# Paired channel tiles, convolution sums in PSUM, MLP weight sums on VectorE and a new GpSimd order in a one-layer hybrid decoder step

## The reference, cut to what matters

```python
def layer(x, s_pool, s_conv, p0, norm1_g, w_in, pool_w, pool_scale, conv_w, w_out, norm2_g, w1, w2):
    hn = rmsnorm(x, norm1_g)
    proj = jnp.einsum('btd,de->bte', hn, w_in)          # 1024 -> [u | B | C | h], 4 x 512
    ya, new_pool = pool_mixer(u, s_pool, p0, pool_w, pool_scale)   # causal means over 2, 4, 8, 16
    yb, new_conv = conv_mixer(bg, cg, hc, s_conv, conv_w)          # B * conv3(C * h)
    mix = jnp.concatenate([ya, yb], axis=-1)
    x = x + jnp.einsum('bte,ed->btd', mix, w_out)
    hn = rmsnorm(x, norm2_g)
    a = jax.nn.relu(jnp.einsum('btd,df->btf', hn, w1))  # 1024 -> 4096
    x = x + jnp.einsum('btf,fd->btd', a * a, w2)        # 4096 -> 1024
    return x, new_pool, new_conv
```

## Time and profile before

| | us |
|---|---|
| median of 3 runs | 713.3 |
| the three runs | 709.56, 713.3, 722.66 |
| the profiled execution | 708.97 |
| its span, slowest core | 707.4 (699.6 to 707.4 over the 8 cores) |
| PE busy | 630.9 (89%), 5430 matmuls |
| DVE busy | 523.2 (74%) |
| ACT busy | 303.9 (43%) |
| POOL busy | 204.6 (29%) |

### The profile page before, as it was taken

The page is one execution under the profiler, slowest core; times in us unless marked ns, Lnnn a source line. Parts: engine busy times, 40 slices in busy tenths (PEclk is TensorE's granted clock), DMA queues, the critical chain, the costliest instruction groups (busy, mean ns, idle before and its releaser), DMA issues.

```text
span 707.4 us, 13629 instructions; the slowest of 8 cores (699.6 to 707.4 us)
## 1 busy us (share of the span) xinstructions
PE 630.9 (89%) x5430; PEld 522.0 (74%) x5430; DVE 523.2 (74%) x1289; ACT 303.9 (43%) x816; POOL 204.6 (29%) x204
## 2 busy tenths in 40 slices
PE   4898896798899588899999996598999999999995
PEld 1486684587678477688888885377878888888895
DVE  2359889589989679737647549957895985976987
ACT  3443352254433345127146054103625735736734
POOL 7078497167638111100000006727220000000001
PEclk9999999899999799999999998799999999999998
DMA  8996295625249977961360466459930450420614
GB/s 211 165 197 143 31 227 143 225 70 184 40 144 192 166 106 215 323 215 35 138 213 5 179 200 110 103 155 184 228 134 2 138 216 2 160 87 1 215 33 123
DMA packets 33983, 100.05 MB, mean 141 GB/s; under 512 B 6720, under 2 KB 17984, under 8 KB 30336
## 3 DMA queue, kind: packets, MB, share of 16 engines
q1 hardware_dynamic: 27072, 71.53, 30.3%
q0 software_dynamic: 6848, 27.66, 23.1%
HBM read 88.13 MB, written 34.11 MB: 173 GB/s over the span
## 4 chain that ended last, share of the span: by engine, by line
PE 56%; DVE 30%; DMA 5%; ACT 4%; issue 3%; POOL 0%; SPq 0%; DVEq 0%
PE psall L574 56%; DVE big L599 17%; DVE big L604 12%; DMA big<-w2p 4%; ACT big L596 3%; DMA big<-x 1%; ACT psall L596 1%; DVE big L850 0%; DVE psall L599 0%; POOL big L599 0%; SPq L617 0%; DVEq L349 0%; DVE big L1125 0%; POOL big L763 0%; DVE big L1148 0%
## 5 line engine op out<-in xcount | busy, mean ns | idle before, releaser
L574 PE MATMUL psall<-big 128*128 128x264 bf16 (+4 forms) x5430 | 630.9, 279 | 69.2 <-DVE big L599 34.5
L574 PEld LDWEIGHTS psall<-big 128*128 128x128 bf16 (+1 forms) x5430 | 522.0, 100 | 178.0 <-DVE big L599 44.2
L599 DVE TENSOR_TENSOR big<-psall,big 128x264 f32<-128x264 f32 (+5 forms) x440 | 174.8, 411 | 119.1 <-PE psall L574 79.5
L599 POOL TENSOR_TENSOR big<-big 128x512 bf16<-128x512 bf16 (+11 forms) x132 | 172.1, 1326 | 299.6 <-DVE big L1148 178.7
L596 ACT ACTIVATE big<-psall 128x264 f32<-128x264 f32 (+3 forms) x404 | 147.0, 384 | 225.6 <-PE psall L574 220.6
L599 DVE TENSOR_TENSOR big<-big 128x264 bf16<-128x264 bf16 (+7 forms) x389 | 178.2, 493 | 35.7 <-ACT big L596 24.4
L596 ACT ACTIVATE big<-big 128x264 bf16<-128x264 f32 (+6 forms) x303 | 139.9, 470 | 144.2 <-DVE big L599 125.9
L604 DVE SCALAR_TENSOR_TENSOR big<-big 128x264 bf16<-128x264 f32 (+4 forms) x264 | 132.3, 533 | 4.6 <-ACT big L596 2.5
L604 DVE SCALAR_TENSOR_TENSOR big<-big,psall 128x264 bf16<-128x264 f32 (+2 forms) x138 | 54.9, 470 | 14.1 <-ACT psall L596 12.5
L617 POOL DMA_DIRECT2D big<-w1p x16 | 9.1, 576 | 144.8 <-PE psall L574 144.8
L596 ACT ACTIVATE psall<-psall 128x264 f32<-128x264 f32 (+3 forms) x108 | 39.1, 375 | 26.1 <-PE psall L574 21.8
(11 more groups left out here) (7 smaller groups left out, 1.8 us busy)
## 6 DMA issues: line engine op xcount, KB each, us to landing
x1d<-big SPq DMA_DIRECT2D x32, 528.0 KB, 5.0
big<-x1d SPq DMA_DIRECT2D x32, 528.0 KB, 4.8
big<-h2d SPq DMA_DIRECT2D x8, 1848.0 KB, 8.1
big<-w1p POOLq DMA_DIRECT2D x16, 512.0 KB, 7.4
big<-w2p POOLq DMA_DIRECT2D x8, 1024.0 KB, 15.5
h2d<-big SPq DMA_DIRECT2D x4, 1848.0 KB, 9.2
yT<-big SPq DMA_DIRECT2D x12, 528.0 KB, 3.2
big<-xg POOLq DMA_DIRECT2D x4, 1056.0 KB, 28.1
```

The lines of the kernel that those rows point to most:

```text
L574: return P.add("tensor", lambda e: e.matmul(out=out.ap, lhsT=lhsT.ap, rhs=rhs.ap, start=start, stop=stop, skip_group_check=skip), [out], [ ...
L599: return P.add(eng, lambda e: e.tensor_tensor(out=out.ap, in0=a.ap, in1=b.ap, op=op), [out], [a, b], cost(eng, out.n, kind))
```

## The change

- Two neighbouring PSUM banks are filled by two tiles (`alloc2`, `ps2`), and one instruction reads both: the copies of u and C, the products with h and with B, the residual add of `w_out`. Banks are handed out least recently freed first, single ones from broken pairs if these are old enough.
- The convolution's running sum stands in PSUM (one bank a channel tile): ScalarE writes it there, the first `stt` reads and writes it, the second reads it and writes `CV`.
- `tsums` is wholly on VectorE.
- `pool_ops`: window 2 is one subtraction straight to `MIX`; each later window writes its own `MIX` row when ready; first additions leave out channel group 0.
- Every GpSimd computation waits for the one before it (a dependency added in `plan`), and the planner keeps VectorE operations with two SBUF operands and GpSimd operations apart (`lock`), with 0.12 us after each GpSimd operation.
- W_in is loaded in pairs, u, C, h, B for channel tiles 0 and 1, then 2 and 3; the first load brings two chunks ahead of x1 and x2.
- `CG` for groups 0 to 2 now lies where the first tile of W1 is loaded later.

```diff
+        op.lock = eng == "gpsimd" or (eng == "vector" and sum(1 for v in ins if v.sb and v.n > 8) > 1)
...
+                if op.lock:
+                    pfree, pown = free[e] + 0.1, e
...
+        g = [o for o in self.order["gpsimd"] if not o.dma]
+        for a, b in zip(g, g[1:]):
+            b.deps.add(a.id)
...
+    def ps2(bb, n, lo=0):
+        v = psall.rearrange("p (a c) -> p a c", a=NBANK)[:, bb[0]:bb[0] + 2, lo:lo + n]
+        return V(v, bank=tuple(bb), n=2 * n)
...
     def alloc():
-        return banks["free"].pop(0)
+        lone = [b for b in banks if (b ^ 1) not in banks]
+        b = min(lone or banks, key=lambda b: banks[b])
+        if lone and min(banks.values()) < banks[b] - 3:
+            b = min(banks, key=lambda b: banks[b])
+        del banks[b]
+        return b
+
+    def alloc2():
+        b = min((b for b in banks if b + 1 in banks), key=lambda b: max(banks[b], banks[b + 1]))
+        del banks[b], banks[b + 1]
+        return b, b + 1
...
-    EO = [0, 1, 2, 3, 8, 12, 9, 13, 4, 10, 14, 5, 11, 15, 6, 7]
+    EO = [0, 2, 8, 12, 4, 10, 14, 6]
...
-    def tsums(W, eng):
-        tt(eng, W[4], W[3], W[0], ALU.subtract, "b")
-        tt("gpsimd", W[3], W[2], W[3], ALU.subtract, "b")
-        tt(eng, W[5], W[2], W[4], ALU.subtract, "b")
-        tt(eng, W[6], W[1], W[5], ALU.subtract, "b")
+    def tsums(W):
+        tt("vector", W[4], W[3], W[0], ALU.subtract, "b")
+        tt("vector", W[5], W[2], W[4], ALU.subtract, "b")
+        tt("vector", W[6], W[1], W[5], ALU.subtract, "b")
+        tt("vector", W[3], W[2], W[3], ALU.subtract, "b")
...
+    def h_pair(g, h):
+        b = win_mm(g, 12 + 2 * h)
+        s = slice(2 * h, 2 * h + 2)
...
+            tt("vector", Z[g][s, 2:266], ps2(b, GN), cg[:, 0:GN], ALU.mult)
...
+        free2(b)
+        cv = cv_of(g, h)
+        for i in range(2):
+            c = 2 * h + i
+            b = alloc()
+            for z, lo, hi, st in ((Z[g], 0, PN, 1), (ZS, PN, GN, 16)) if g == 7 else ((Z[g], 0, GN, 1),):
+                m = hi - lo
+                t = ps(b, m, lo)
+                act(t, z[c, 2 * st:2 * st + m], AF.Copy, scale=cn(28 + 8 + c))
+                stt(t, z[c, st:st + m], cn(28 + 4 + c), t, ALU.mult, ALU.add)
+                stt(cv[i, lo:hi], z[c, 0:m], cn(28 + c), t, ALU.mult, ALU.add)
+            free(b)
...
+        for d in range(0, 8, 2):
+            b = alloc2()
...
+            x = XT[g][d:d + 2, o:o + GN]
+            tt("vector", x, ps2(b, GN), x, ALU.add)
+            free2(b)
+            act(q[d:d + 2], x, AF.Square)
```

More of the change, by code:

```diff
@@ L128, in add @@
         for v in ins:
-            if v.bank is not None:
-                banks[v.bank] = banks.get(v.bank, False)
+            for b in v.bank:
+                banks[b] = banks.get(b, False)
         for v in outs:
-            if v.bank is not None:
-                banks[v.bank] = True
+            for b in v.bank:
+                banks[b] = True
         for b, w in banks.items():
@@ L235, in schedule @@
                     engs.add(ENGS[i])
-            for e in engs:
-                if free[e] > t + 1e-9 or not heaps[e]:
+            if "vector" in engs or "gpsimd" in engs:
+                engs |= {"vector", "gpsimd"}
+            for e in ENGS:
+                if e not in engs or free[e] > t + 1e-9 or not heaps[e]:
                     continue
-                _, i = heapq.heappop(heaps[e])
+                h = heaps[e]
+                i = None
+                if e in ("vector", "gpsimd") and pfree > t + 1e-9 and pown != e:
+                    skipped = []
+                    while h:
+                        x = heapq.heappop(h)
+                        if ops[x[1]].lock:
+                            skipped.append(x)
+                        else:
+                            i = x[1]
+                            break
+                    for x in skipped:
+                        heapq.heappush(h, x)
+                    if i is None:
+                        heapq.heappush(evs, (pfree, cnt, 1, ENGS.index(e)))
+                        cnt += 1
+                        continue
+                else:
+                    i = heapq.heappop(h)[1]
                 op = ops[i]
@@ L472, in build_nc @@
     o += 4480
[L473 to L478, removed]
+    CG = [T(o, (2, 280), F32)]
+    o += 2240
     assert o <= AREA, (o, AREA)
@@ L524, in build_nc @@
     o += 4256
[L525 to L530, removed]
+    CV.append(T(o, (2, GN), F32))
+    o += 2112
     assert o <= W1o + 5 * 7168
@@ L623, in build_nc @@
     finals = []
-    banks = {"free": list(range(NBANK))}
+    banks = {b: b - NBANK for b in range(NBANK)}
+    clock = [0]
     def alloc():
-        return banks["free"].pop(0)
+        lone = [b for b in banks if (b ^ 1) not in banks]
[8 more added lines that the diff above has]
+        return b, b + 1
     def free(b):
-        banks["free"].append(b)
+        clock[0] += 1
+        banks[b] = clock[0]
     def cn(i):
@@ L657, in build_nc @@
     load_x(2)
-    for i in range(1, 16):
+    for i in range(1, 8):
         load_win(i)
@@ L807, in w_out, with b_pair @@
+    def b_pair(g, h):
+        b = win_mm(g, 4 + 2 * h, xoff(g))
+        s = slice(4 + 2 * h, 6 + 2 * h)
+        tt("vector", MIX[g][s], ps2(b, GN), cv_of(g, h)[:, 0:GN], ALU.mult)
+        free2(b)
     def w_out(g):
@@ L878, in front @@
             dma("sync", ZS[:, 0:32], dr(scT), 128 * 128 * 4, tag="sc")
-        for c in range(4):
-            u_chunk(g, c)
+        u_pair(g, 0)
+        u_pair(g, 1)
         pool_ops(g)
```

180 lines of the change are left out of this document (83 added, 97 removed).

## The result

The changed kernel takes 689.06 us (685.79 to 691.08), against 709.56 and 713.30 for the kernel before beside it; the ratio is 0.968, with a 95% interval from 0.960 to 0.976. It is 3.2% faster. The profiled executions, against which the sum was made, are 708.97 and 685.79 us: -23.2 us, where -35 was forecast.

A forecast was written before the change was run, and what follows sets the result against it. VectorE, slowed beside GpSimd on operations with two SBUF operands, was taken to bound the front and a short MLP stretch. -4 - 17 - 14 = -35 us against 708.97 gave 674 us, range 652 to 702.

The forecast's parts named there:

- The case's own range: Whole kernel: the forecast's main case, 655 to 685 us, given a chance of 0.67.
- VectorE's time in the front: 77 to 290 us: VectorE's busy time falls from 180.2 to 165.3 us, while PE needs 165.8.
- Pairs: 77 to 290 us: two tiles per instruction make 52 instructions fewer, at 0.10 us each, -5.2 us of VectorE time.
- the 14 us taken: 77 to 290 us: VectorE time slowed beside GpSimd that would go, with 0 and 22.7 us as ends.
- the switch: 420 to 500 us, second half of the weights: contention goes wholly with sums on VectorE, -14 us, ends -24 and -6.
- I take the share that the bounding engine reaches now, 84.6%: Stage length as PE's needed time over 84.6%: 196 us for 77 to 290 us, 65.7 for 420 to 500 us.
- the 17 us: 77 to 290 us: forecast gain of the stage, 213 to 196 us, ends +5 and -33 us.
- From 0 to 77 us: Start of the kernel: cheaper convolution sums against a later first product with h, -4 us, ends -7 and +4.
- The first rival: 77 to 290 us: pairs and leftover contention eat the front's gain, 14 to 17 us, about 690 us; chance 0.14.
- The landings rival: All 24 weight loads: VectorE waits for late landings, 1.4 us each, 34 us, about 707 us; chance 0.12.
- Banks: 16 h pairs: PE waits 4.1 us each for banks held by convolution sums, 66 us, 740 in all; chance 0.07.
- The rule weighed there: Pairs, 77 to 290 us: larger operations help a saturated engine, smaller ones otherwise; the sum took the first half, -5.2 us.

The follow-up runs named there:

- the order: Kernel after with the next group's normalisation, n1_ss(g+1), recorded ahead of the Winograd pair b_pair(g,0): 690.60 us, ratio 0.972.
- the sums alone: Kernel before with only the weight sums of every W1 and W2 chunk moved to VectorE: 685.41 us, ratio 0.963.
- the sums and the split alone: Kernel before with all weight sums on VectorE and the store of h2 in two parts: 674.82 us.
- the kernel after with everything: Kernel after with next group's normalisation first, h2 store in two parts, W2[1]'s sums behind w_out(7), and w_out(7) read bank by bank: 674.79 us.
- other parts alone: Kernel after with the weight sums put back on GpSimd: 706.71 us, ratio 0.995.

## Why the prediction was right, and where it was not

The verdict (faster) and the range held; the number was 12 us low, by its own account: -35 forecast, -23.2 measured. The case's own range, 655 to 685, was missed.

- **VectorE's time in the front: right in the sum.** 165.3 us forecast, 161.2 measured. Pairs saved 2 x 0.40 - 0.69 = 0.11 us each (0.10 taken); the 1056-column sums came to 0.73 us (0.8 taken). Two prices were too low, the convolution's `stt` with 0.46 us and not 0.41, and the 512-column weight sums with 0.60 and not 0.37, together some 8 us. More contention went than the 14 us taken: the 1056- and 528-column sums alone fell from 41.8 to 26.2 us, and 16 `stt` in SBUF that the sum had left out from 9.6 to 6.4 us. The price of 0.37 was of a VectorE alone; that is what they cost at the switch, while in the front GpSimd was at work beside them.
- **The step that failed: "I take the share that the bounding engine reaches now, 84.6%".** It turned VectorE's and PE's busy time into a stage's length, and it was wrong both ways. In the front PE's needed time came to 1450 x 0.113 = 164 of 213 us, 77%, in place of 196 us; at the switch PE reached 98%, and the stage gave 22.7 us and not 14. Two errors, -17 us too much and 8.7 us too little, left the total near; that was luck. Busy shares don't say what ends a stage. In the front PE stood for VectorE as long as before, and at the longest stands VectorE itself stood, in its fixed order, for the store of h2 and for W2[1]: taking both away gave 8.9 us, and with the order and single banks at `w_out(7)` too 13.6 us (688.36 to 674.79). What keeps the rest of the 17 us was not tried. The share of before already held such waits (1.6 and 1.7 us), and the step let them shrink with VectorE's work; in the kernel after they were 4.0 and 2.3 us.
- **What could have been read beforehand.** The row of `stt` has it: idle 1.6 us for h2d, and the earlier trace rows has a wait of 8.0 us for line 604. The text took that wait for VectorE's load, and mostly it was: of the 8.0 us VectorE stood for 1.6. The rows gave the sign, not the size. In the kernel after VectorE came to this place 4.5 us earlier, and the store ended only 3.5 us earlier.

```profile
237.35 3.29 DVE L604 SCALAR_TENSOR_TENSOR big<-big,psall 128x264 bf16<-128x264 f32 x8 [1.61 <-DMA h2d<-big]
240.69 13.94 PE L574 MATMUL psall<-big 128*128 128x264 bf16 x104 [8.02 <-DVE big L604]
```

- **The switch: right in its mechanism.** Where the sums run decides; the sums alone carry the gain (0.963) and the rest without them almost none (0.995). Contention went wholly, as said; VectorE waited 5.7 us there for the loads' landings, and PE stood 1.6 us in all, 16.2 before.
- **From 0 to 77 us:** -4 forecast, 413 - 394 = 19 matmuls, 2.1 us, measured.
- **The first rival** gave 690 us, the time that came, and its sign came too: PE's waits as long as before with VectorE less busy. Its mechanism is not what was found: contention did go, and pairs cost PE turns where only one pair is free, at `w_out(7)`; with single banks there alone nothing changed, for the late transfers covered it. **The landings rival** has a part of the mechanism (a sum that waits for a load, and bank sums behind it), though at one place of 24; beside the load there is the store (VectorE stood 4.0 us for the store and 2.3 for the load in one profile of the kernel after, 0.9 and 7.0 in the other).
- **Banks**: right in its mechanism and in its sign, PE waiting for line 632, and too large in its price. The convolution sums hold their banks behind VectorE's bursts, but PE stood for that once a group, 2.3 to 3.1 us, and once 7.06 us with the store in front, not 4.1 us at each of 16 h pairs. With the normalisation first these stands fell to 1.7 or 1.8 us. What the sums in PSUM cost as a whole was not tried alone.
- **The rule weighed there** (the Trainium skill, Perfetto Trace Analysis, section Optimizing Scalar/DVE Operations): larger operations for a saturated engine, smaller ones where it isn't and the large ones make bubbles. What the runs show goes with its second half: with both waits out of the way the kernel with pairs and sums in PSUM has VectorE busy 166.3 us from 77 to 290 us and takes 679.46 us, the one with single banks and SBUF sums 184.1 us and 673.36 us. Less VectorE time did not buy time. The two kernels differ in more than the size of operations (order, loads, spacing), so the rule itself was not tried.

Three kernels are level at the end: weight sums on VectorE, the store in two parts and W2[1]'s sums held, 673.36 us; the sums and the split alone, 674.82; and the kernel after with everything, 674.79. All are 2% below the kernel after, and the first two have little of the change.

## What to carry to other kernels

Busy time saved on an engine becomes time only if that engine's work is what ends the stage; before pricing it, follow the longest waits back through the engine to what it waited for itself. On an engine that works in order, an operation that needs a transfer holds up everything recorded behind it: put the sums that free PSUM ahead of it, and do not overwrite a buffer whose store may still run. When removing one wait changes nothing, remove the next one with it before dropping the theory.

## What the runs showed of the hardware

- A store of 1848 KB whose page median is 8.4 us took 18.3 us before, 21.0 after and 26.8 with the earlier order, when it ran beside the first W2 load, with x1's rows and small outputs. In that stretch of the kernel after size counted little: the 4 KB of `ncpT` took 14.2 us to land.
- VectorE's `bf16` sums with all operands in SBUF follow what GpSimd does beside them: 1056 columns took 1.12, 0.96, 0.84 and 0.74 us on the mean (before; sums alone; other parts alone; after). GpSimd was busy 106, 60, 97 and 55 us: they were shorter where it had less work, and shorter again in the two kernels where its work is spaced.
